# Up and gate products of four feed-forward layers in pairs by Strassen's scheme (Winograd's form)

## The chip, the cores and the metric

One core of one Trainium2 chip. The metric is the device time of one execution in microseconds, the median of the runs shown.

## The reference, cut to what matters

A float32 model on 512 tokens of width 1024: two hybrid layers (feed-forward, a mixer of delta rule, window attention and cross attention over 256 memory rows, feed-forward, each with a layer norm after it), then one block of another kind with four attentions and a convolutional feed-forward. The change touches the four feed-forward layers of the first part, in which `d_ff` is 2816:

```python
def swiglu(x, w_gu, w_down):
    gate, up = jnp.split(x @ w_gu, 2, axis=-1)
    return (jax.nn.silu(gate) * up) @ w_down
...
h = layer_norm(DEEPNORM_ALPHA * x + 0.5 * swiglu(x, ffn1_w_gu, ffn1_w_down), ln_g[0], ln_b[0])
...
return layer_norm(DEEPNORM_ALPHA * h + 0.5 * swiglu(h, ffn2_w_gu, ffn2_w_down), ln_g[2], ln_b[2])
```

## The kernel before, in words

Activations lie transposed, features on the partitions: an activation of width 1024 is 8 tiles ("pages", 128 partitions x 512 tokens), the hidden layer of a feed-forward 22. Weights come in blocks of 128 x 128. The precision of float32 is kept with rounded operands: each operand is split into a rounded part (`w_hi`, `X.hi`) and the rest (`w_lo`, `X.lo`), and a block is multiplied by three matmuls of 512 columns, hi x hi, hi x lo and lo x hi (`block_matmuls`, L2134, L2135, L2143). Eight PSUM banks hold the results.

The blocks of all layers form one stream, `weights`, in slabs of four blocks (`SLAB`, 256 KB). The program is made by a planner (`Order`) that runs once over the whole model and records every operation in the order in which each engine's queue then holds it. `place` (L478) hands out the next block and with it keeps the stream going: SP loads the slab 7 ahead (`load_slab`), ScalarE rounds the slab 4 ahead (`round_slab`, L2441), VectorE subtracts to get the rest, over the raw weights (`rest_slab`, L2822). The slab buffers are taken in turn: 7 raw ones and 5 rounded ones.

`ffn` (L771) goes over 22 pairs of output tiles, the gate tile j and the up tile 22 + j. Each is a `product` of 8 blocks into a bank. Two products later `ffn_act` turns the pair into one page of the hidden layer: ScalarE silu out of the gate's bank (L2512), VectorE times the up bank (L2969), ScalarE rounds (L2515), VectorE subtracts (L2972). `update` (L652) then multiplies by `down` (8 products of 22 blocks) and adds into the residual R (`add_up`, L2840). Norms and other side work are generators that step between the blocks (`Pace`); in the first feed-forward the norm of the memory rows and their key and value products (`prepare_memory`) run beside the up and gate products. `half_matmuls` (L2153 to L2155) is the last product of the program, in two halves of 256 columns.

```python
for m in range(len(open_pairs), FT):
    pair = []
    for n in (m, FT + m):
        if open_pairs:
            taken_in(j)
            j += 1
        pair.append(self.bg.straight(self.product(up, n, X), beside=True))
    open_pairs.append(pair)
```

Of the kernel before, what the change touches and what calls it, by code (L numbers as in the profile page):

```python
# [13 lines left out]
P = 128  # L14
# [19 lines left out]
NSLAB = 1120  # L34
NRAW = 7
NHI = 5
AHEAD = NHI - 1
# [3 lines left out]
PAGES = 82  # L41
CONST_PARTS = 4
NGAIN = 48

# [60 lines left out]
class Lane:  # L105
# [3 lines left out]
    def __init__(self, sems):  # L109
        self.tensor, self.scalar, self.vector = sems  # L110
        self.raised = [0, 0, 0]


class Marks(dict):
# [5 lines left out]
    def will(self, tensor="", scalar="", vector=""):  # L120
        lane = self.lane
        for k, (sem, names) in enumerate(((lane.tensor, tensor), (lane.scalar, scalar), (lane.vector, vector))):
            for name in names.split():
                lane.raised[k] += 1
                self[name] = (sem, lane.raised[k])
        return self


class Slot:
# [3 lines left out]
    def __init__(self, f, r=None):  # L133
        self.f, self.r, self.free, self.full = f, r, (), None

# [6 lines left out]

class Stock:


    def __init__(self, slots):
        self.slots = list(slots)

    def take(self):
        return self.slots.pop(0)  # L150

    def give(self, slot, *signals):
        slot.free = signals
        self.slots.append(slot)


class Operand:
# [3 lines left out]
    def __init__(self, tiles=None):  # L161
        self.tiles = tiles
        self.hi, self.lo, self.ready, self.pages = [], [], [], []

# [193 lines left out]
LANES = ("setup load norm ffn proj conv decay unit head0 head1 gate finish merge cross window soft0 soft1 "  # L358
# [3 lines left out]
class Memory:  # L362


    def __init__(self, nc, ctx, w, x_t, mem_t, consts, params, table, buckets, out):
# [5 lines left out]

        self.nc, self.w, self.x_t, self.mem_t, self.consts, self.params = nc, w, x_t, mem_t, consts, params
        self.table, self.buckets, self.out = table, buckets, out
        with nc.sbuf_tensor("w_lo", [P, NRAW, SLAB * P], F32R) as lo:
            self.w_lo = lo
        self.raw = sb("raw", [P, NRAW, SLAB * P])
        self.w_hi = sb("w_hi", [P, NHI, SLAB * P], F32R)
# [15 lines left out]
        self.lane_sems = {k: tuple(sem(f"{k}_{e}") for e in ("tensor", "scalar", "vector")) for k in LANES}  # L393
# [18 lines left out]
class Order:  # L412
# [5 lines left out]

    set_constants = load_constants = constants_ready = load_slab = round_slab = rest_slab = idle
# [19 lines left out]
    def __init__(self, memory):  # L439
# [3 lines left out]
        self.pages = Stock([Slot(f, r) for f, r in memory.page_aps])  # L443
        self.bg = Pace()
        self.order = []
        self.freed, self.multiplied = {}, 0
# [14 lines left out]

    def loaded(self, s):
        while self.next_raw <= min(s, NSLAB - 1):
            self.load_slab(self.next_raw)
            self.next_raw += 1

    def rounded(self, s):
        while self.next_round <= min(s, NSLAB - 1):
            self.round_slab(self.next_round)
# [3002 lines left out]
```

## Time and profile before

| what | value |
|---|---|
| time, median of 3 runs | 3622.58 us (3621.11 to 3623.22) |
| profiled execution: span | 3619.4 us |
| TensorE busy | 3578.4 us, 99% |
| weight loads busy | 2873.9 us, 79% |
| VectorE, ScalarE, GpSimd busy | 54%, 42%, 0% |
| DMA mean | 85 GB/s |

The times are of whole executions on the device. The profiled execution's own time is not listed beside them; what stands is its span, from its first to its last instruction, 3.2 us below the median. The page gives busy time by engine, a strip of 40 slices, the chain that ended last and the costliest groups of instructions; the trace can be asked for one line, one stretch or one engine in order of time. A matmul's end is modelled, and matmuls overlap, so the distance between two starts is what one costs.

### The profile page before, as it was taken

What the parts mean: (1) busy time and instruction counts of PE and PEld (TensorE: products, weight loads), DVE (VectorE), ACT (ScalarE), POOL (GpSimd) and SP (SyncE); (2) the same over time, 40 slices, a digit from 0 to 9 for tenths busy, and PEclk for the clock granted to TensorE, in tenths of its full rate; (3) what the DMA queues carried; (4) which work ended last, traced back from release to release, by engine and by line L of the source; (5) the groups of instructions that cost most, each with busy time, mean ns of one, the idle gap of its engine ahead of it and who ended that gap; (6) DMA issues with size and microseconds to landing.
All of it is one profiled execution on the core that took longest, in us unless ns stands there. A gap on an engine that the chain in (4) does not pass through costs nothing.

```text
span 3619.4 us, 44083 instructions
## 1 busy us (share of the span) xinstructions
PE 3578.4 (99%) x16952; PEld 2873.9 (79%) x16952; DVE 1945.8 (54%) x3781; ACT 1523.3 (42%) x2957; POOL 0.2 (0%) x4
## 2 busy tenths in 40 slices
PE   9999999999999999999999999999999999999999
PEld 7888878877888888888878877888886777788887
DVE  5333555556753345334655566733456787666643
ACT  4433354554443234333455543533335443444432
POOL 0000000000000000000000000000000000000000
PEclk9999999999999999999999999999999999999999
DMA  4443332112333333333321123333323222233333
GB/s 149 120 113 94 88 90 56 41 50 69 95 88 96 94 94 89 95 93 94 90 72 49 42 59 85 89 95 93 94 85 88 65 64 85 76 94 95 94 93 90
DMA packets 170600, 308.14 MB, mean 85 GB/s; under 512 B 19030, under 2 KB 23287, under 8 KB 170392
## 3 DMA queue, kind: packets, MB, share of 16 engines
q1 hardware_dynamic: 169624, 304.54, 29.8%
q8 instruction: 135, 2.21, 0.3%
q10 hardware_dynamic: 768, 0.79, 0.1%
q14 instruction: 73, 0.60, 0.1%
HBM read 300.27 MB, written 4.72 MB: 84 GB/s over the span
## 4 chain that ended last, share of the span: by engine, by line
PE 95%; DVE 2%; ACT 2%; issue 0%; DMA 0%; DVEq 0%; ACTq 0%
PE bank L2134 28%; PE bank L2143 28%; PE bank L2135 28%; PE bank L2122 2%; PE bank L2117 1%; PE bank L2195 1%; PE bank L2288 1%; PE bank L2298 1%; PE bank L2163 1%; PE bank L2215 0%; PE bank L2386 0%; PE bank L2208 0%; PE bank L2142 0%; PE bank L2236 0%; PE bank L2359 0%
## 5 line engine op out<-in xcount | busy, mean ns | idle before, releaser
L2134 PE MATMUL bank<-page_r,w_hi 128*128 128x512 f32 x4470 | 1788.1, 400 | 16.7 <-DVE w_lo L2822 9.6
L2143 PE MATMUL bank<-page_r,w_lo 128*128 128x512 f32 x4470 | 1765.9, 395 | 0.0
L2135 PE MATMUL bank<-page_r,w_hi 128*128 128x512 f32 x4470 | 1755.8, 393 | 0.0
L2441 ACT ACTIVATE w_hi<-raw 128x512 fp32r<-128x512 f32 x1120 | 697.2, 628 | 1022.0 <-PE bank L2143 1018.1
L2134 PEld LDWEIGHTS bank<-page_r,w_hi 128*128 128x128 f32 x4470 | 842.4, 188 | 220.6 <-issue 17.7
L2143 PEld LDWEIGHTS bank<-page_r,w_lo 128*128 128x128 f32 x4470 | 842.3, 188 | 191.9
L2135 PEld LDWEIGHTS bank<-page_r,w_hi 128*128 128x128 f32 x4470 | 842.2, 188 | 189.4 <-issue 3.6
L2822 DVE TENSOR_TENSOR w_lo<-raw,w_hi 128x512 fp32r<-128x512 f32 x1120 | 747.9, 687 | 417.8 <-ACT w_hi L2441 415.7
L2969 DVE TENSOR_TENSOR page_f<-page_f,bank 128x512 f32<-128x512 f32 x88 | 60.6, 688 | 322.6 <-PE bank L2143 276.1
L2840 DVE SCALAR_TENSOR_TENSOR page_f<-bank,page_f 128x512 f32<-128x512 f32 x64 | 44.2, 691 | 168.3 <-PE bank L2143 167.7
L2515 ACT ACTIVATE page_r<-page_f 128x512 fp32r<-128x512 f32 x88 | 55.7, 633 | 177.2 <-DVE page_f L2969 177.2
L2472 ACT ACTIVATE page_f<-page_f 128x512 f32<-128x512 f32 (+1 forms) x81 | 48.6, 604 | 126.9 <-DVE page_f L2840 113.4
L2569 ACT ACTIVATE page_f<-bank 128x256 f32<-128x256 f32 (+3 forms) x144 | 49.6, 388 | 123.8 <-PE bank L2122 123.4
L3291 DVE SCALAR_TENSOR_TENSOR page_f<-bank,par,page_f 128x511 f32<-128x511 f32 x88 | 65.4, 748 | 59.5 <-ACT page_f L2782 57.9
L2972 DVE TENSOR_TENSOR page_r<-page_f,page_r 128x512 fp32r<-128x512 f32 x88 | 60.9, 692 | 63.4 <-ACT page_r L2515 63.4
L2122 PE MATMUL bank<-cst,page_f 128*128 128x128 f32 x580 | 89.2, 275 | 5.7 <-DVE page_r L2828 4.7
L2122 PEld LDWEIGHTS bank<-cst,page_f 128*128 128x128 f32 x580 | 69.8, 143 | 23.7 <-DVE page_r L2828 5.5
L2977 DVE SCALAR_TENSOR_TENSOR page_f<-page_f,bank 128x512 f32<-128x512 f32 x80 | 54.8, 685 | 54.0 <-PE bank L2143 53.6
L2559 ACT ACTIVATE page_f<-bank 128x512 f32<-128x512 f32 x80 | 47.3, 592 | 54.0 <-PE bank L2143 53.8
L3045 DVE SCALAR_TENSOR_TENSOR page_f<-bank,par,page_f 128x511 f32<-128x511 f32 (+2 forms) x72 | 53.8, 748 | 23.7 <-ACT page_f L2611 22.0
L2195 PEld LDWEIGHTS bank<-page_f 128*64 128x64 f32 (+1 forms) x592 | 46.9, 148 | 23.1 <-issue 17.6
L2117 PE MATMUL bank<-page_f 128*128 128x128 f32 x512 | 65.2, 275 | 0.0
(251 smaller groups left out, 2507.4 us busy)
## 6 DMA issues: line engine op xcount, KB each, us to landing
raw<-weights SPq DMA_DIRECT2D x1120, 256.0 KB, 2.6
page_f<-x_t SPq DMA_DIRECT2D x8, 256.0 KB, 5.7
bias_rows<-page_f SPq DMA_DIRECT2D x8, 256.0 KB, 2.0
page_f<-bias_rows SPq DMA_DIRECT2D x8, 256.0 KB, 3.2
out_t<-page_f SPq DMA_DIRECT2D x12, 128.0 KB, 1.8
cst<-consts SPq DMA_DIRECT2D x4, 272.0 KB, 3.5
page_f<-mem_t SPq DMA_DIRECT2D x8, 128.0 KB, 3.3
bias_rows<-page_f SPq DMA_DIRECT2D x8, 64.0 KB, 1.9
```

What stands on the lines that cost most here:

```text
L2117: last = self.e.matmul(b.tile(i), x, y, start=True, stop=True)
L2122: last = self.e.transpose(b.tile(i), ap[:, i * P:(i + 1) * P], self.const("ident"))
L2134: self.e.matmul(o, hi, X.hi[kt], start=first, stop=False)
L2135: self.e.matmul(o, hi, X.lo[kt], start=False, stop=False)
L2143: last = self.e.matmul(o, lo, X.hi[kt], start=False, stop=final)
L2195: last = self.e.matmul(out.f[rows, i * P:(i + 1) * P], v, q.tile(kb), start=kb == 0, stop=kb == len(parts) - 1)
L2441: self.e.activation(self.m.w_hi[:, s % NHI, :], self.m.raw[:, s % NRAW, :], ACT.Copy) \
L2515: self.e.activation(h.r[:, :], s.f[:, :], ACT.Copy).then_inc(k.lane.scalar, 1)
L2822: self.e.tensor_tensor(self.m.w_lo[:, s % NRAW, :], self.m.raw[:, s % NRAW, :], self.m.w_hi[:, s % NHI, :].bitcast(F32), ALU.subtract).the ...
L2969: self.e.tensor_tensor(s.f[:, :], s.f[:, :], lift.f[:, :], ALU.mult).then_inc(k.lane.vector, 1)
L2972: self.e.tensor_tensor(l.r[:, :], s.f[:, :], h.r[:, :].bitcast(F32), ALU.subtract).then_inc(k.lane.vector, 1)
L3291: self.e.scalar_tensor_tensor(out=p.f[:, sh:], in0=b.f[:, 0:SEQ - sh], scalar=self.col("conv2", (2 - sh) * 2 * FT + m), in1=p.f[:, sh:], o ...
```

## The change

17 of the 22 pairs of each of the four layers (j = 5 to 21, 68 in all) are now made by Strassen's scheme in Winograd's form, in two stretches: 6 pairs, then the part of the `down` product that needs the hidden tiles 0 to 10, then 11 pairs, then the rest of `down`. The first 5 pairs stay as they were ("lone products").

For a pair the output is cut into 2 x 2: gate or up tile, tokens 0 to 255 or 256 to 511; the inner dimension is cut into k tiles 0 to 3 and 4 to 7. The weights are four quarters of 512 columns: a11 (gate, k 0 to 3), a21 (up, k 0 to 3), a22 (up, k 4 to 7), a12 (gate, k 4 to 7). There are 7 products of 4 blocks, each block 3 matmuls of 256 columns, where there were 16 blocks of 3 matmuls of 512:

- weights s1 = a21 + a22 and s3 = a21 + a11: one GpSimd instruction of 1024 columns, `sum_bottom`. s2 = s1 + a11 and s4 = s2 + a12: VectorE, 512 columns each (`sum_second`, `sum_fourth`). Signs lie in the sums of X.
- rounding on ScalarE: a11 (h11, 512 columns), s1 and s3 (h13), s2 and s4 (h24), a12 and a22 (h12), 1024 columns each. The rests on VectorE alike: l11, l13, l24, l12.
- sums of X, four per k tile, made once per layer (`sums_of`), in 16 pages.
- TensorE, in this order within a cycle: q1 (a11), q5 (s1), q4 of the pair before (a22), q6 (s2), q3 (s4), q2 (a12), q7 (s3). Products add up in PSUM: ScalarE copies q1 into q6's bank (`seed`), and keeps q5 (`p5`) and q6 (`u2`) in a page; VectorE adds `c12` (after q3) and `c22` (after q7, awaited by q4), multiplies with the two halves of silu (`h2`, `h1`), and ScalarE and VectorE round the page and take its rest.
- the preparation of a pair is cut into 9 steps (`prepare`), which stand between the products of the pair before and its own.

Raw buffers are 14 and rounded ones 9, of which 7 and 4 may be lent as pages; pages are 71 in place of 82. `prepare_memory` moves, with the loads of the constants and of the memory rows on SP, from the up and gate products of the first layer to the second part of its `down` product. The preparation of the first pair of a stretch (its "head") stands between the blocks of the last lone products, or of the first part of `down`.

```diff
-NSLAB = 1120
-NRAW = 7
-NHI = 5
+NSLAB = 1120 - 4 * 68
+NPAIR = 68
+NRAW = 14
+NHI = 9
+LOADED = 7
+LENT = {"raw": 7, "hi": 4}
-PAGES = 82
+PAGES = 71
...
+    def pair_product(self, p, name, bank, first, *after):
+        hi, lo, ready = p.units.pop(name)
+        p.k.will(tensor=name)
+        self.pair_matmuls(p.k, bank, first, hi, lo, ready, after, p.operands(name))
...
+            if cur:
+                k = cur.k
+                self.pair_product(cur, "q1", cur.a, True)
+            if prev:
+                self.pair_lift(prev.k, prev.b, prev.t)
+                self.pair_join(prev.k, prev.t, prev.s)
+            if cur:
+                step(cur)
+                self.pair_product(cur, "q5", cur.c, True)
+                self.pair_seed(k, cur.a, cur.b)
+                step(cur)
+            step(nxt)
+            if prev:
+                self.pair_product(prev, "q4", prev.b, False, prev.k["c22"])
+            if cur:
+                self.pair_keep(k, "p5", k["q5"], cur.c, cur.t, 0)
+                step(cur)
+                self.pair_product(cur, "q6", cur.b, False, k["seed"])
+            step(nxt)
+            if prev:
+                self.pair_last(prev.k, prev.b, prev.s)
+            if cur:
+                self.pair_product(cur, "q3", cur.c, False, k["p5"])
+                self.pair_keep(k, "u2", k["q6"], cur.b, cur.t, 1)
+            if prev:
+                self.pair_round(prev.k, prev.s, h)
+            step(nxt)
+            if cur:
+                self.pair_product(cur, "q2", cur.a, False, k["seed"])
+                self.pair_first(k, cur.c, cur.t, cur.s)
+            step(nxt)
+            if prev:
+                self.pair_rest(prev.k, prev.s, h, l)
+            if cur:
+                self.pair_product(cur, "q7", cur.b, False, k["u2"])
+                self.pair_gate(k, cur.a, cur.s)
+            step(nxt)
+            step(later)
...
+    def pair_matmuls(self, k, b, first, hi, lo, ready, after, xs):
+        for mark in after:
+            self.wait_ge(*mark)
+        self.wait_ge(*ready)
+        for kt, (x_hi, x_lo, x_ready) in enumerate(xs):
+            c = slice(kt * P, kt * P + P)
+            self.wait_ge(*x_ready)
+            self.e.matmul(b.cols(256), hi.r[:, c], x_hi, start=first and kt == 0, stop=False,
+                          skip_group_check=not first)
+            self.e.matmul(b.cols(256), hi.r[:, c], x_lo, start=False, stop=False, skip_group_check=not first)
+            last = self.e.matmul(b.cols(256), lo.r[:, c], x_hi, start=False, stop=kt == 3,
+                                 skip_group_check=not first)
...
+class Pool(Engine):
+    def sum_bottom(self, p, low, high, a21, out):
+        for unit in (low, high, a21):
+            self.wait_ge(*unit.full)
+        two = low.region.rearrange("p (u c) -> p u c", c=UNIT)[:, low.at:high.at + 1:step, :]
+        twice = a21.f.rearrange("p (o c) -> p o c", o=1).broadcast_to([P, 2, UNIT])
+        self.e.tensor_tensor(out[0].wide().rearrange("p (u c) -> p u c", c=UNIT), two, twice, ALU.add) \
```

VectorE's queue in the steady part of a layer's up and gate products, before (one pair; `page_f36` is the gate's page, `w_lo` a slab's rest, `blocks_multiplied` TensorE's count):

```order
L2822 TENSOR_TENSOR w_lo<-raw,w_hi 128x512 [waits slab_rounded] x7
L2969 TENSOR_TENSOR page_f36<-page_f36,bank4 128x512 [waits blocks_multiplied,ffn_scalar]
L2972 TENSOR_TENSOR page_r38<-page_f36,page_r37 128x512 [waits ffn_scalar,norm_vector]
L2822 TENSOR_TENSOR w_lo<-raw,w_hi 128x512 [waits slab_rounded] x8
L2969 TENSOR_TENSOR page_f76<-page_f76,bank1 128x512 [waits blocks_multiplied,ffn_scalar]
```

The same queue now, one cycle of the second stretch of the first layer (`prep_` and `pair_` are semaphores of the preparation and of the pairs; in order: second sum, l11, c12, fourth sum, rest of the page before, l13, c22, h2, l24 and l12, h1):

```order
L3215 TENSOR_TENSOR raw<-raw 128x512 [waits prep_pool]
L3230 TENSOR_TENSOR w_lo<-raw,w_hi 128x512 [waits prep_scalar]
L3259 TENSOR_TENSOR page_f36<-page_f26,bank7 128x256 [waits pair_scalar,pair_tensor]
L3221 TENSOR_TENSOR raw<-raw 128x512 [waits prep_vector,slab_landed6]
L3281 SCALAR_TENSOR_TENSOR page_r43<-page_f42,page_r37 128x512 [waits pair_scalar]
L3227 TENSOR_TENSOR w_lo<-raw,w_hi 128x1024 [waits prep_scalar]
L3264 TENSOR_TENSOR page_f26<-page_f26,bank1 128x256 [waits pair_tensor]
L3270 TENSOR_TENSOR page_f36<-page_f36,page_f26 128x256 [waits pair_vector,pair_scalar]
L3227 TENSOR_TENSOR w_lo<-raw,w_hi 128x1024 [waits prep_scalar] x2
L3276 TENSOR_TENSOR page_f36<-page_f36,bank1 128x256 [waits pair_tensor,pair_scalar]
```

Where a pair had four slab rests and two gate instructions of 512 columns, it now has eleven instructions, three of them of 1024 columns, and each waits for work of another engine or of its own in the same cycle.

ScalarE's queue in the same cycle (u2, round of the page before, h11, h13, silu of both halves, h24, h12, seed, p5):

```order
L2817 ACTIVATE page_f26<-bank1 128x256 [waits pair_tensor]
L2830 ACTIVATE page_r37<-page_f42 128x512 [waits pair_vector]
L2799 ACTIVATE w_hi<-raw 128x512 [waits slab_landed8]
L2797 ACTIVATE w_hi<-raw 128x1024 [waits prep_pool]
L2822 ACTIVATE page_f36<-page_f36 128x256 [waits pair_vector]
L2824 ACTIVATE page_f36<-bank2 128x256 [waits pair_tensor]
L2797 ACTIVATE w_hi<-raw 128x1024 [waits prep_vector]
L2797 ACTIVATE w_hi<-raw 128x1024 [waits slab_landed7,slab_landed6,pair_tensor]
L2812 ACTIVATE bank4<-bank5 128x256 [waits pair_tensor]
L2817 ACTIVATE page_f44<-bank3 128x256 [waits pair_tensor]
```

The round of the page and h11 now stand behind u2, and h13 ahead of the silu.

ScalarE's queue at the end of the first stretch (last p5 and u2, round of the page before, silu of both halves, round of the last page, then the slabs of the down product):

```order
L2817 ACTIVATE page_f42<-bank3 128x256 [waits pair_tensor]
L2817 ACTIVATE page_f42<-bank4 128x256 [waits pair_tensor]
L2830 ACTIVATE page_r52<-page_f70 128x512 [waits pair_vector,ffn_vector]
L2822 ACTIVATE page_f49<-page_f49 128x256 [waits pair_vector]
L2824 ACTIVATE page_f49<-bank0 128x256 [waits pair_tensor]
L2830 ACTIVATE page_r56<-page_f49 128x512 [waits pair_vector]
L2788 ACTIVATE w_hi<-raw 128x512 [waits slab_landed12]
L2788 ACTIVATE w_hi<-raw 128x512 [waits slab_landed10]
L2788 ACTIVATE w_hi<-raw 128x512 [waits slab_landed11]
```

The first slab of the down product is rounded only after the last pair's page. Before, slabs were rounded all the way from one product to the next.

## Rows read from the trace of the kernel before

**Rows 1.** The page, busy time by engine, and granted clock by slice

```profile
PE 3578.4 (99%) x16952; PEld 2873.9 (79%) x16952; DVE 1945.8 (54%) x3781; ACT 1523.3 (42%) x2957; POOL 0.2 (0%) x4
...
PEclk9999999999999999999999999999999999999999
```

**Rows 2.** The page, chain that ended last, by engine and by line

```profile
PE 95%; DVE 2%; ACT 2%; issue 0%; DMA 0%; DVEq 0%; ACTq 0%
PE bank L2134 28%; PE bank L2143 28%; PE bank L2135 28%; PE bank L2122 2%; PE bank L2117 1%; PE bank L2195 1%; PE bank L2288 1%; PE bank L2298 1%; PE bank L2163 1%; PE bank L2215 0%; PE bank L2386 0%; PE bank L2208 0%; PE bank L2142 0%; PE bank L2236 0%; PE bank L2359 0%
```

**Rows 3.** Groups by shape, TensorE: xcount | busy us, mean ns | idle before

```profile
L2134 PE MATMUL bank<-page_r,w_hi 128*128 128x512 f32 x4342 | 1752.1, 404 | 16.7 <-DVE w_lo L2822 9.6 <-DVE page_f L3026 3.2 <-DVE page_r L2964 2.5
```

**Rows 4.** Who waited for whom: us in total, times, longest us

```profile
ACT w_hi L2441 <- PE bank L2143: 1018.1, 607, 5.2
...
DVE page_f L2969 <- PE bank L2143: 276.1, 66, 6.1
```

**Rows 5.** Busy time of each engine, steady feed-forward stretch

```profile
core 0: us, PE busy (x) PEld busy (x) DVE busy (x) ACT busy (x) POOL busy (x), PEclk, DMA share, GB/s
1500.00:1600.00 100.00, 100.00 (x430) 80.53 (x429) 35.03 (x54) 31.21 (x53) 0.00 (x0) 1.00 0.34 95
```

**Rows 6.** Timeline, TensorE, last product: start us, us, line, form

```profile
3602.86 0.28 PE L2153 MATMUL bank<-page_r,w_hi 128*128 128x256 f32 x1
3602.97 0.28 PE L2154 MATMUL bank<-page_r,w_hi 128*128 128x256 f32 x1
...
3608.42 0.28 PE L2155 MATMUL bank<-page_r,w_lo 128*128 128x256 f32 x1
```

**Rows 7.** Timeline, weight loads, same product

```profile
3602.98 0.19 PEld L2155 LDWEIGHTS bank<-page_r,w_lo 128*128 128x128 f32 x1
3603.10 0.19 PEld L2153 LDWEIGHTS bank<-page_r,w_hi 128*128 128x128 f32 x1
```

**Rows 8.** Groups by shape, VectorE

```profile
L2822 DVE TENSOR_TENSOR w_lo<-raw,w_hi 128x512 fp32r<-128x512 f32 x1120 | 747.9, 687 | 417.8 <-ACT w_hi L2441 415.7
...
L2977 DVE SCALAR_TENSOR_TENSOR page_f<-page_f,bank 128x512 f32<-128x512 f32 x80 | 54.8, 685 | 54.0 <-PE bank L2143 53.6
...
L3026 DVE SCALAR_TENSOR_TENSOR page_f<-bank,cst 128x256 f32<-128x256 f32 x48 | 18.3, 420 | 66.0 <-PE bank L2215 66.0
```

**Rows 9.** Groups by shape, ScalarE

```profile
L2441 ACT ACTIVATE w_hi<-raw 128x512 fp32r<-128x512 f32 x1120 | 697.2, 628 | 1022.0 <-PE bank L2143 1018.1 <-DMA raw<-weights 3.2 <-issue 0.2
...
L2512 ACT ACTIVATE page_f<-bank 128x512 f32<-128x512 f32 x88 | 51.1, 581 | 0.1
...
L2569 ACT ACTIVATE page_f<-bank 128x256 f32<-128x256 f32 x92 | 31.6, 382 | 82.8 <-PE bank L2122 82.6
...
L2569 ACT ACTIVATE page_f<-bank 128x512 f32<-128x512 f32 x12 | 6.5, 596 | 8.6 <-PE bank L2122 8.6
```

**Rows 10.** Busy time of each engine, first stretch

```profile
0.00:53.00 53.00, 47.54 (x196) 38.27 (x197) 22.57 (x40) 26.19 (x44) 0.20 (x4) 1.00 0.59 184
```

**Rows 11.** Timeline, one steady gate, all engines

```profile
1199.52 0.40 PE L2134 MATMUL bank<-page_r,w_hi 128*128 128x512 f32 x1
...
1199.79 0.69 DVE L2969 TENSOR_TENSOR page_f<-page_f,bank 128x512 f32<-128x512 f32 x1 [4.25 <-PE bank L2143]
...
1200.51 0.63 ACT L2515 ACTIVATE page_r<-page_f 128x512 fp32r<-128x512 f32 x1 [2.42 <-DVE page_f L2969]
...
1201.05 0.61 ACT L2441 ACTIVATE w_hi<-raw 128x512 fp32r<-128x512 f32 x1
...
1201.24 0.69 DVE L2972 TENSOR_TENSOR page_r<-page_f,page_r 128x512 fp32r<-128x512 f32 x1 [0.77 <-ACT page_r L2515]
...
1201.85 1.29 DVE L2822 TENSOR_TENSOR w_lo<-raw,w_hi 128x512 fp32r<-128x512 f32 x2
```

**Rows 12.** DMA issues by line: KB each, median us to landing

```profile
raw<-weights SPq DMA_DIRECT2D x1120, 256.0 KB, 2.6
```

**Rows 13.** One line, L2155: durations, first and last start

```profile
L2155 PE MATMUL bank<-page_r,w_lo x20: 276/280/285, 3603.1 to 3610.3; 128*128 128x256 f32 x20
```

More of the change, by code:

```diff
@@ L40 @@
 HALF = (slice(0, 256), slice(256, 512))
-PAGES = 82
+PAGES = 71
 CONST_PARTS = 4
 NGAIN = 48
+UNIT = SLAB * P
+ALONE = 5
+FIRST = 11
+QUARTERS = ("a11", "a21", "a22", "a12")
 BLOCK_US = 0.7
@@ L772, in ffn @@
+    def ffn(self, source, X, up, down, scale, early, after, scaled=None, mem=None):
         H = Operand()
-        pairs = [m for j in range(3) for m in (j, FT + j)]
+        pairs = [m for j in range(ALONE) for m in (j, FT + j)]
+        self.until(len(pairs) * DT)
         if early:
             first = self.bg.got(self.bg.begin(source, X, [early.product(up, m) for m in pairs[:2]],
-                                              [self.product(up, m, X) for m in pairs[2:]], early.made))
+                                              [self.product(up, m, X) for m in pairs[2:6]], early.made))
@@ L793, in taken_in @@
             self.pages.give(s, k["rest"])
-        j = 0
-        for m in range(len(open_pairs), FT):
-            pair = []
+        if scaled:
+            self.bg.get(scaled)
+        sums = self.bg.add(self.sums_of(X, 1.0 / ALPHA))
+        head = self.pair(up, ALONE, FT + ALONE)
+        for m in range(len(open_pairs), ALONE):
+            made = []
             for n in (m, FT + m):
                 if open_pairs:
-                    taken_in(j)
-                    j += 1
-                pair.append(self.bg.straight(self.product(up, n, X), beside=True))
-            open_pairs.append(pair)
@@ L804, in ffn @@
-        while open_pairs:
-            taken_in(j)
-            j += 1
-        if scaled:
-            self.bg.get(scaled)
-        return self.update(down, H, scale, Spread(self, after, after.count == 2))
+                    taken_in()
+                w = Later(self.product(up, n, X))
+                while not w.done:
+                    self.bg.tell(w)
+                    self.bg.steps(1)
+                    if m == ALONE - 1 and not w.done and (n > FT or self.next_block % DT in (2, 5)):
+                        head.step(until=6)
@@ new lines, in ffn, with ahead @@
+                made.append(w.value)
+            open_pairs.append(made)
+        self.bg.get(sums)
+        while open_pairs:
+            taken_in()
+        def ahead(blocks):
+            self.until(blocks)
+            s = self.next_block // SLAB
+            for i in range(LOADED - 1):
+                self.loaded(s + i)
+            yield
+            self.rested(s + 2)
+        head.step(until=6)
+        self.paired(up, range(ALONE, FIRST), X, H, head, ahead(FIRST * DT))
+        part, H = H, Operand()
@@ new lines, in ffn @@
+        head = self.pair(up, FIRST, FT + FIRST)
+        left = FIRST * DT
+        for m in range(DT):
+            w = Later(self.product(down, m, part))
+            while not w.done:
+                self.bg.tell(w)
+                left -= 1
+                if left in (24, 20, 12, 9, 6, 3):
+                    head.step()
+            k = self.marks("norm").will(vector="sum")
+            self.add_up(k, w.value, m, scale)
+            self.Rt[m] = k["sum"]
+            self.banks.give(w.value, k["sum"])
@@ L811, in project @@
+        self.drop(part, w.value.full)
+        self.paired(up, range(FIRST, FT), X, H, head, ahead(NSLAB * SLAB))
+        self.drop(X, (self.lanes["pair"].tensor, self.lanes["pair"].raised[0]))
+        return self.update(down, H, scale, Spread(self, after, after.count == 2), k0=FIRST, beside=mem)
     def project(self, mat, mt, X, n=512, product=None):
@@ L3379, in _ @@
             Vector(e, memory).run()
-    return plan.order
+        @block.gpsimd
+        def _(e):
+            Pool(e, memory).run()
+    return plan.order, plan.pair_order
 def pad_cols(a, n):
```

433 lines of the change are left out of this document (371 added, 62 removed).

## The prediction

> **What bounds the kernel now.** I read the page's busy shares first: TensorE is busy for 3578.4 of 3619.4 us, VectorE for 54%, ScalarE for 42%, GpSimd not at all, and the granted clock is full in all 40 slices [rows 1]. The chain that ended last says the same: PE 95%, 28% on each of the three matmul lines [rows 2]. The groups by shape show that TensorE hardly waits: 16.7 us ahead of 4342 matmuls of the costliest form [rows 3]. So what counts is how many matmul columns are issued, and where TensorE is made to wait. The longest waits are ScalarE's and VectorE's for TensorE, 1018.1 us of one line [rows 4]: those engines have room, and idle time there is free.
>
> **The price of TensorE's work.** In steady feed-forward work 430 matmuls of 512 columns start in 100 us, 0.2326 us each, while VectorE is busy 35.03 us of the 100 [rows 5]. For 256 columns with a weight load before each, I take the last product: its first matmul starts at 3602.86 and the 48th at 3608.42, so 5.56/47 = 0.1183 us each [rows 6]. The loads there start 0.12 us apart and last 0.19, so they overlap one another [rows 7]; a load does not hold the short matmuls back.
> - Removed per pair: 16 blocks x 3 matmuls = 48 x 0.2326 = 11.16 us.
> - Added per pair: 7 products x 4 blocks x 3 = 84 x 0.1183 = 9.94 us, 1.42 per product.
> - 68 pairs x 1.225 = **-83.3 us** on the path. All other matmuls stay.
>
> **Does the rest keep up inside a stretch?** Prices [rows 8, 9]: VectorE 0.69 us for 512 columns, 0.42 for 256, so 1.04 ns a column and 1.22 for 1024 (an estimate from the two); ScalarE 0.63, 0.38 and, with 0.84 ns a column from its 596 and 382 ns, 1.06.
> - VectorE per pair: four of 512 (second sum, rest of a11, fourth sum, rest of the page) 2.76, three of 1024 (rests) 3.66, four of 256 (c12, c22, two multiplications) 1.68: 8.10 of 9.94 us, where before it had 35.03% of 11.16 = 3.9.
> - ScalarE: two of 512, three of 1024, five of 256: 6.34 us.
> - DMA: four quarters of 256 KB in 9.94 us, 105 GB/s; the start of the program ran at 184 [rows 10].
> - The sums of X, per layer: VectorE 4 x (4 x 0.42 + 2 x 0.69) = 12.2 us, under 10 lone products of 8 x 0.70 us. Cover 56 us, cost 0.
>
> Both fit in sum, but they are queues, so the tight loop has to be followed. Handovers come from one steady gate [rows 11]: TensorE to VectorE 0.27 us after the next product's first matmul (1199.52 to 1199.79), VectorE to ScalarE 0.03, ScalarE to VectorE 0.10; an instruction that is ready starts 0.08 (VectorE) or 0.09 (ScalarE) before the last one ends. From the end of q6: 0.27; u2 0.29; the previous pair's round 0.54; h11 of the next pair 0.63 + 0.10; on VectorE l11 0.61, c12 0.34, fourth sum 0.61, rest of the page 0.61, l13 1.22 + 0.03. That is 5.25 us, and only then may q5 of the next pair start. Between lie q3, q2, q7 and q1: 5.68 us. **Room 0.43 us**, cost 0; without any overlap it would be 5.75, 0.07 too long, over the 60 transitions (68 pairs less the first of each of 8 stretches) 4 us. The other handovers (seed, p5, c22, h1) have two products, 2.84 us, between writer and reader.
>
> **GpSimd's sum** has no row: the trace has only four memsets, 0.2 us together [rows 1]. Below it is bounded by VectorE's 1.22 us, above I allow four times that, 4.9; nearest is VectorE's row, and I take twice it, 2.4 us, for an engine that has only done memsets here. It waits for a22, whose transfer is issued when q7 of the pair before is done and takes 2.6 us [rows 12]: start at 2.8 us of the cycle, end 5.2, and the second sum has until 6.9. Cost 0. The Trainium skill (GPSIMD Engine Reference, Performance versus the Vector engine) has 4497 ns for an add of 2048 fp32 columns, thus an estimated 2.25 for this one; by it the sum is the same, and no run here shows it yet.
>
> **The ends of stretches** are where TensorE must wait; eight of them (6 and 11 pairs per layer, four layers). After the last q7, q4 waits for c22: 0.27 + 0.42 + 0.05 = 0.74. After q4 the down product waits for its first slab, whose rounding is queued behind the pair's own: 0.27, h1 0.42 + 0.03, round 0.54, slab round 0.63, then the slab's rest behind the page's rest on VectorE, which starts at 0.27 + 0.45 + 0.63 + 0.10 = 1.45 and lets the next one in 0.61 later: 2.06 + 0.69 + 0.05 = 2.8. Together 3.5 x 8 = **+28 us**; bounds 0 and 5 each. At the four entries after lone products the last gate (silu 0.58, times, round, rest) stands ahead of l24 and the seed: l24 ends 0.27 + 0.58 + 0.69 + 0.63 + 0.69 + 1.22 = 4.1 us after the last lone product, q6 could start at 2.84: 1.3 x 4 = **+5**. The entries from the middle of the down product have no gate: 0.
>
> **Once, in layer 1**: constants and memory (2.4 MB) are now queued on SP behind the last pair, and VectorE waits for them after five slab rests, 14 us of cover. At 184 GB/s [rows 10] they take 13 us, then the memory's norm starts, on whose mean TensorE waits: **+3**, bounds 0 and 8. Fewer pages (71, with 7 + 4 lent): 0, since the lenders are idle outside the stretches; if not, waits for pages would show in the mixers.
>
> **Sum**: 3619.4 - 83.3 + 28 + 5 + 3 = 3572.1 for the profiled execution; the median of the runs lies 3.2 above its span, thus **3575 us**.
>
> **The rivals.**
> 1. *VectorE and GpSimd hold each other up (slower).* If a GpSimd sum of length P starts at 2.8, just before l12, and VectorE must wait it out, then l12 (1.14), h1 (0.42 + 0.03) follow, and the round starts at P + 4.39 instead of 5.68 + 0.56 = 6.24. Less the room of 0.43 this costs P - 2.28 us per transition. At P = 2.4 that is 7 us in all; it decides from P = 3.06, where 60 x 0.78 eats the 47 won; at 3.5 it is 73 us, 3648. For it: VectorE would have 8.10 + P = more than 9.94 us. Against: l12 may get in first, then GpSimd waits instead and the room stays. It rests on the Trainium skill (SBUF — State Buffer, Who interferes with whom), which says that a VectorE instruction with two SBUF inputs and a GpSimd instruction reading SBUF block each other for the whole instruction; no row here can agree or not. Slower outright 12%; a milder form (P to 3, 3598 to 3618) 18%.
> 2. *The short matmuls do not reach 0.1183 us.* The stretch I took has no change of accumulator that waits. All sixty of that kind, from 3602.86 to 3610.3 [rows 6, 13], stand (3610.3 - 3602.86)/59 = 0.126 apart, with the norm's own matmuls and a wait among them. At that price: 68 x 84 x 0.0077 = 44 us more, 3619. Against it, the 47 intervals are even, and each block of four already changes its weights. 5%.
> 3. *The ends cost little*, if slabs were rounded earlier than the queues read: 3545. 6%.
> 4. *The products come, but the alone part stalls* for the sums or the heads, 5 us per layer: 3595. In the forecast's range.
>
> **How the numbers follow.** Forecast (TensorE the bound, 3552 to 3598) 59%, milder lock 18%, slower 12%, short matmuls 5%, cheap ends 6%. The range 3552 to 3616 leaves out the slower case and part of the cheap ends. A measurement of this kernel tells 0.2%, 7 us, from no change: faster by more (below 3615) 83%, within 5%, slower 12%.
>
> **What would show it.** 5712 matmuls of 256 columns on the pair line, 0.118 us apart; GpSimd with 68 instructions of some 2.4 us; VectorE busy about 80% in a stretch of pairs; TensorE's idle time, 41 us now, about 36 larger, at eight places of 3.5 us; a pair every 9.9 us. Wrong if the pair's period is 10.5 us or more, if VectorE's rests of 1024 last over 1.3 us while GpSimd is busy, or if TensorE idles before q5 or q7 in every pair.

## The result: the changed kernel is 0.17% slower, where 1.3% faster was predicted

| what | before | after |
|---|---|---|
| time, median of 20 runs each | 3622.07 us (3618.35 to 3623.91) | 3628.55 us (3624.96 to 3629.78) |
| ratio | | 1.0017, 95% interval 1.0011 to 1.0024 |
| profiled span | 3619.4 us | 3627.2 us |

The predicted time was 3575 us with a range of 3552 to 3616. The page of the changed kernel, busy time and clock, the chain that ended last, and the groups of TensorE's two first matmul lines (L2465 opens a block of 512 columns, L2500 one of 256 in a pair):

```profile
PE 3520.6 (97%) x19400; PEld 2952.2 (81%) x19400; DVE 2319.9 (64%) x4249; ACT 1691.5 (47%) x3259; POOL 200.9 (6%) x72
...
PEclk9999999999999999999999999999999999999999
...
PE 89%; DVE 7%; ACT 3%; issue 1%; DMA 0%; SPq 0%; DVEq 0%; ACTq 0%
...
L2465 PE MATMUL bank<-page_r,w_hi 128*128 128x512 f32 (+1 forms) x3382 | 1365.2, 404 | 45.1 <-DVE w_lo L3210 37.9
...
L2500 PE MATMUL bank<-page_r,w_hi 128*128 128x256 f32 x1904 | 539.7, 283 | 29.7 <-DVE w_lo L3230 15.1
```

Against [rows 1 to 3]: TensorE's share of the chain fell from 95% to 89%, VectorE's rose from 2% to 7%, and the idle time ahead of the two lines is 75 us where it was 17 ahead of one. In both cases what came last is a rest made by VectorE (`w_lo`). PE busy fell by 58 us, not by 83; part of the difference is slower work, below. Where does it wait? Windows of 100 us inside two stretches of pairs, with the columns of [rows 5]:

```profile
core 0: us, PE busy (x) PEld busy (x) DVE busy (x) ACT busy (x) POOL busy (x), PEclk, DMA share, GB/s
1200.00:1300.00 100.00, 100.00 (x847) 100.00 (x846) 85.10 (x110) 58.10 (x99) 28.71 (x9) 1.00 0.31 96
1020.00:1030.00 10.00, 10.00 (x44) 8.05 (x43) 9.85 (x15) 6.87 (x12) 0.00 (x0) 1.00 0.28 83
...
1060.00:1070.00 10.00, 4.95 (x23) 4.27 (x22) 8.55 (x10) 4.93 (x8) 2.41 (x1) 0.71 0.00 1
200.00:300.00 100.00, 99.01 (x837) 98.85 (x836) 84.05 (x109) 58.14 (x99) 27.57 (x9) 1.00 0.31 96
```

Inside a stretch it goes as foreseen: 847 matmuls start in 100 us, 0.118 us each, so a pair takes 84 x 0.118 = 9.9 us. The time is lost outside: from 1060 to 1070 us, where the second feed-forward layer goes from its lone products to its first pair, TensorE is busy for 4.95 us of 10, at a granted clock of 0.71. Forty microseconds earlier, where VectorE makes the norm beside the lone products, it is busy 9.85 us of 10 (6.45, 9.05, 9.85 and 4.96 in the four windows from 1000 to 1040 us). The timeline of TensorE at that entry (a number in brackets is idle time before, and what ended it):

```profile
1058.85 0.50 PE L2465 MATMUL bank<-page_r,w_hi 128*128 128x512 f32 x1 [1.19 <-DVE w_lo L3210]
...
1061.52 0.40 PE L2474 MATMUL bank<-page_r,w_lo 128*128 128x512 f32 x1
1066.96 0.55 PE L2500 MATMUL bank<-page_r,w_hi 128*128 128x256 f32 x1 [5.05 <-DVE w_lo L3230]
...
1067.75 0.41 PE L2500 MATMUL bank<-page_r,w_hi 128*128 128x256 f32 x1
1068.39 0.41 PE L2500 MATMUL bank<-page_r,w_hi 128*128 128x256 f32 x1
```

5.44 us lie between the last lone matmul and q1, and then one block of three takes 0.64 us instead of 0.355. With the wait at 1058.85 and a late q6 this entry costs 10.3 us, and the two in the other later layers 9.5 and 10.3. What VectorE and GpSimd do meanwhile (same timeline; L3238 to L3251 are the sums of X, L3428 and L3431 a lone gate, L3210 a slab's rest, L3215 the second sum, L3230 the rest of a11):

```profile
1047.60 0.41 DVE L3238 TENSOR_TENSOR page_f<-page_f 128x256 f32<-128x256 f32 x1
...
1051.64 1.29 DVE L3251 SCALAR_TENSOR_TENSOR page_r<-page_f,page_r 128x512 fp32r<-128x512 f32 x2
1052.85 0.69 DVE L3210 TENSOR_TENSOR w_lo<-raw,w_hi 128x512 fp32r<-128x512 f32 x1
...
1060.17 0.68 DVE L3428 TENSOR_TENSOR page_f<-page_f,bank 128x512 f32<-128x512 f32 x1
1061.55 0.69 DVE L3431 TENSOR_TENSOR page_r<-page_f,page_r 128x512 fp32r<-128x512 f32 x1 [0.70 <-ACT page_r L2903]
1062.05 2.41 POOL L3780 TENSOR_TENSOR raw<-raw 128x1024 f32<-128x1024 f32 x1 [15.53 <-PE bank L2474]
1062.16 3.45 DVE L3251 SCALAR_TENSOR_TENSOR page_r<-page_f,page_r 128x512 fp32r<-128x512 f32 x2
1065.54 0.68 DVE L3215 TENSOR_TENSOR raw<-raw 128x512 f32<-128x512 f32 x1
1066.14 0.68 DVE L3230 TENSOR_TENSOR w_lo<-raw,w_hi 128x512 fp32r<-128x512 f32 x1
```

VectorE is still making sums of X when the lone products are over. And one instruction pair, L3251 x2, takes 1.29 us at 1051.64 and 3.45 us at 1062.16, while GpSimd's sum runs. Groups by shape over the whole kernel:

```profile
L3227 DVE TENSOR_TENSOR w_lo<-raw,w_hi 128x1024 fp32r<-128x1024 f32 x204 | 309.0, 1542 | 0.0
L3780 POOL TENSOR_TENSOR raw<-raw 128x1024 f32<-128x1024 f32 x68 | 200.7, 2951 | 2404.6 <-PE bank L2474 1249.0 <-DMA raw<-pairs 866.2 <-PE bank L2503 289.4
...
L3251 DVE SCALAR_TENSOR_TENSOR page_r<-page_f,page_r 128x512 fp32r<-128x512 f32 x32 | 31.5, 1024 | 0.4 <-ACT page_r L2804 0.4
L3276 DVE TENSOR_TENSOR page_f<-page_f,bank 128x256 f32<-128x256 f32 x68 | 28.2, 415 | 28.8 <-PE bank L2503 28.8
```

Rests of 1024 columns (L3227) take 1.54 us on average where 1.22 was estimated. The last line is h1, which reads one operand from SBUF and one from a bank: 25 of its 68 executions lie wholly inside a GpSimd sum and take 420 to 422 ns, no more than others do. The end of a stretch (windows, then timeline; 1309.68 is the first block of the down product's second part in the second layer):

```profile
1306.90:1309.60 2.70, 0.21 (x2) 0.01 (x1) 1.69 (x4) 1.93 (x4) 0.00 (x0) 1.00 0.96 321
1310.00:1313.30 3.30, 3.30 (x9) 2.56 (x8) 2.04 (x4) 0.90 (x2) 0.00 (x0) 0.50 0.98 347
```

```profile
1309.68 0.61 PE L2465 MATMUL bank<-page_r,w_hi 128*128 128x512 f32 x1 [2.57 <-DVE w_lo L3210]
1310.94 0.63 PE L2465 MATMUL bank<-page_r,w_hi 128*128 128x512 f32 x1
1312.22 0.63 PE L2465 MATMUL bank<-page_r,w_hi 128*128 128x512 f32 x1
```

The wait is as forecast, eight times (L3210 makes the rest that ends it; L2788's rounding of the slab, at 1308.21 us, follows ScalarE's own last instruction without a wait for a transfer). But then the granted clock is 0.50, the lower of the two levels (1.2 in place of 2.4 GHz), and a block takes 1.27 us instead of 0.70. This follows six of the eight ends and costs some 1.5 us each.

### The profile page after: what moved, and what is told of

It is laid out like the page before. It is cut to its first block, busy times and chain, and to the rows that moved or that the text cites. A ratio compares the mean times of both kernels' runs of the same rounds, so it can differ in the third digit from the quotient of the medians.

```text
span 3627.2 us, 49995 instructions
## 1 busy us (share of the span) xinstructions
PE 3520.6 (97%) x19400; PEld 2952.2 (81%) x19400; DVE 2319.9 (64%) x4249; ACT 1691.5 (47%) x3259; POOL 200.9 (6%) x72
## 4 chain that ended last, share of the span: by engine, by line
PE 89%; DVE 7%; ACT 3%; issue 1%; DMA 0%; SPq 0%; DVEq 0%; ACTq 0%
PE bank L2465 21%; PE bank L2474 20%; PE bank L2466 20%; PE bank L2500 6%; PE bank L2503 5%; PE bank L2502 5%; PE bank L2453 2%; PE bank L2448 1%; PE bank L2543 1%; DVE w_lo L3227 1%; PE bank L2636 1%; DVE page_r L3251 1%; PE bank L2646 1%; DVE w_lo L3210 1%; PE bank L2511 1%
## 5 line engine op out<-in xcount | busy, mean ns | idle before, releaser
L2465 PE MATMUL bank<-page_r,w_hi 128*128 128x512 f32 (+1 forms) x3382 | 1365.2, 404 | 45.1 <-DVE w_lo L3210 37.9
L2474 PE MATMUL bank<-page_r,w_lo 128*128 128x512 f32 (+1 forms) x3382 | 1339.5, 396 | 0.0
L2466 PE MATMUL bank<-page_r,w_hi 128*128 128x512 f32 (+1 forms) x3382 | 1330.0, 393 | 0.0
L2465 PEld LDWEIGHTS bank<-page_r,w_hi 128*128 128x128 f32 x3382 | 641.5, 190 | 205.5 <-DVE w_lo L3210 44.0
L2788 ACT ACTIVATE w_hi<-raw 128x512 fp32r<-128x512 f32 x848 | 521.6, 626 | 598.3 <-PE bank L2474 593.9
L2466 PEld LDWEIGHTS bank<-page_r,w_hi 128*128 128x128 f32 x3382 | 641.5, 190 | 140.0 <-issue 3.6
L3210 DVE TENSOR_TENSOR w_lo<-raw,w_hi 128x512 fp32r<-128x512 f32 x848 | 563.0, 687 | 129.5 <-ACT w_hi L2788 129.1
L2500 PE MATMUL bank<-page_r,w_hi 128*128 128x256 f32 x1904 | 539.7, 283 | 29.7 <-DVE w_lo L3230 15.1
L2502 PE MATMUL bank<-page_r,w_hi 128*128 128x256 f32 x1904 | 537.5, 282 | 0.0
L2503 PE MATMUL bank<-page_r,w_lo 128*128 128x256 f32 x1904 | 537.3, 282 | 0.0
L2500 PEld LDWEIGHTS bank<-page_r,w_hi 128*128 128x128 f32 x1904 | 361.5, 190 | 34.8 <-issue 23.0
L2502 PEld LDWEIGHTS bank<-page_r,w_hi 128*128 128x128 f32 x1904 | 361.5, 190 | 0.2
L3780 POOL TENSOR_TENSOR raw<-raw 128x1024 f32<-128x1024 f32 x68 | 200.7, 2951 | 2404.6 <-PE bank L2474 1249.0
L3227 DVE TENSOR_TENSOR w_lo<-raw,w_hi 128x1024 fp32r<-128x1024 f32 x204 | 309.0, 1542 | 0.0
L2797 ACT ACTIVATE w_hi<-raw 128x1024 fp32r<-128x1024 f32 x204 | 213.2, 1054 | 27.4 <-DVE raw L3221 16.3
```

The costliest lines, as they stand in the source:

```text
L2465: self.e.matmul(o, hi, X.hi[kt], start=first, stop=False)
L2466: self.e.matmul(o, hi, X.lo[kt], start=False, stop=False)
L2474: last = self.e.matmul(o, lo, X.hi[kt], start=False, stop=final)
L2500: self.e.matmul(b.cols(256), hi.r[:, c], x_hi, start=first and kt == 0, stop=False, skip_group_check=not first)
L2502: self.e.matmul(b.cols(256), hi.r[:, c], x_lo, start=False, stop=False, skip_group_check=not first)
L2503: last = self.e.matmul(b.cols(256), lo.r[:, c], x_hi, start=False, stop=kt == 3, skip_group_check=not first)
```

## The experiments

Three causes stood out: the ends of stretches, the entries, and GpSimd's sum. Each was changed alone on the changed kernel (3628.55 us), then together. Times are medians; each ratio is to the kernel before, timed again with each group of runs (3622.55, 3623.25 and 3623.1 us), with its 95% interval.

**Ends: three slabs of the down product made earlier.** The generator `ahead` has two steps: it loads slabs, then it rounds three of them and takes their rests. They stood at the end of the last pair's cycle and at the end of the one behind it, which only finishes that pair. Now both stand inside the last pair's cycle, behind q4 of the pair before and ahead of q7:

```diff
+            if cur and not nxt:
+                next(ahead, None)
...
+            if cur and not nxt:
+                next(ahead, None)
             if cur:
                 self.pair_product(cur, "q7", cur.b, False, k["u2"])
...
-            if not nxt:
-                next(ahead, None)
```

> The first three slabs of the down product are loaded, rounded and rested inside the last pair's cycle, ahead of its q7, where they stood behind its page. Theory A (the stretches of pairs run as foreseen; what is lost stands at their ends and entries, each wait with a piece of half clock behind it): the 2.85 us between the last q4 and the first down block fall to under 0.5 at all eight ends, -20 to -22 us, and the pieces of half clock behind six of them go too, -1.5 us each, so some 3600 us. Theory B (VectorE is the bound and work that is put earlier comes back as another wait): under 5 us won, and q3, q7 or q4 of the last pairs start late instead.

Measured: 3597.41 us, ratio 0.9933 (0.992 to 0.9945), 31 less. TensorE at the first end (timeline): only the wait of q4 for c22 is left, and the down product (L2467) follows q4 (L2502 to L2505) at once.

```profile
127.22 0.42 DVE L3266 TENSOR_TENSOR page_f<-page_f,bank 128x256 f32<-128x256 f32 x1
...
127.70 0.39 PE L2502 MATMUL bank<-page_r,w_hi 128*128 128x256 f32 x1 [0.51 <-DVE page_f L3266]
...
129.10 0.28 PE L2505 MATMUL bank<-page_r,w_lo 128*128 128x256 f32 x1
129.22 0.40 PE L2467 MATMUL bank<-page_r,w_hi 128*128 128x512 f32 x1
```

So the 2.8 us behind each q4 come from where these steps stand in the queues, and the gap of 0.5 us that is left is followed by the full clock, eight times of eight. The entries stay at 10.6, 9.8 and 10.2 us.

**GpSimd's sum on VectorE.** `sum_bottom` as it stands, in VectorE's queue; GpSimd does nothing.

```diff
-        k.will(pool="bottom")
+        k.will(vector="bottom")
```

> The sum s1, s3 of each pair moves from GpSimd to VectorE; GpSimd does nothing. If GpSimd's reads stop VectorE's instructions with two SBUF inputs: the rests of 1024 columns fall from 1.54 us to 1.22, the five stalls of 1.2 us inside stretches go (6 us), and the three late entries lose 2 us each: -12 us, some 3616, although VectorE has 68 x 1.22 = 83 us more to do. If the long rests have another cause (ScalarE, DMA): they stay at 1.54, and VectorE's further 1.22 us per pair bring the pair's period over 9.94 us, 10 to 40 us slower.

Measured: 3602.86 us, ratio 0.995 (0.9938 to 0.9963), 26 less, though VectorE has 68 more instructions. By shape, the rests (first) and the sum (second):

```profile
L3238 DVE TENSOR_TENSOR w_lo<-raw,w_hi 128x1024 fp32r<-128x1024 f32 x204 | 242.8, 1218 | 0.0
L3220 DVE TENSOR_TENSOR raw<-raw 128x1024 f32<-128x1024 f32 x68 | 82.8, 1218 | 1.7 <-DMA raw<-pairs 1.5 <-issue 0.3
```

The rests fall from 1542 to 1218 ns: 204 x 0.324 = 66 us that VectorE had lost; the sum costs it 83. The direction was expected, the size was twice the expected one: the stalls in the middle of stretches (5 us) and the 1.1 us at the four entries from the down product went, the three late entries fell from 10 to 7 us, and the first layer's by 2. Another 4 us of the gain in the profiled execution is that three of the eight ends are followed by a piece of half clock, where six were; nothing in the edit explains that, so what the edit itself gives lies nearer 22 us than 26.

**Six lone pairs in place of five** (64 pairs by the scheme), on the changed kernel:

```diff
-ALONE = 5
+ALONE = 6
```

> Six lone pairs of output tiles per layer in place of five, 64 Strassen pairs in place of 68. It gives back 4 x 1.22 = 5 us of TensorE's gain and gives VectorE 7 us more per layer ahead of the first stretch. If the late entries (10 us each in three layers) come from VectorE's backlog of norm, sums of X and gates: q1 of the first stretch starts within 1 us of the last lone product, -7 to -9 us each, in sum 17 to 22 us faster than the change, some 3608. If they come from the loads of the head or from GpSimd alone: the entries stay near 10 us and it is 5 us slower, 3633.

Measured: 3618.02 us, ratio 0.9987 (0.9977 to 0.9996), 10.5 less, about half of what was expected. q1 now follows the last lone product without a gap, but the slabs' rests ahead of it come late (timeline):

```profile
1057.00 0.50 PE L2465 MATMUL bank<-page_r,w_hi 128*128 128x512 f32 x1 [2.10 <-DVE w_lo L3210]
...
1063.30 0.50 PE L2465 MATMUL bank<-page_r,w_hi 128*128 128x512 f32 x1 [0.43 <-DVE w_lo L3210]
```

VectorE's queue is full there, and one more lone pair moves part of the wait rather than removing it.

**TensorE kept busy behind q4.** 24 matmuls of 128 columns on a constant into a spare bank, behind the last q4, in all layers but the first; their results are used by nobody.

```diff
+            if prev and not cur and self.filling:
+                self.fill_matmuls(prev.k, spare, 24)
```

> 24 matmuls of 128 columns on a constant, into a spare bank, behind the last q4 of each stretch in all layers but the first (six ends); nothing else changes, and their results are used by nobody. They last 2.6 us at full clock, inside the wait of 2.85. If idleness lowers the clock: no piece of half clock behind those six ends (four have one now), -1.5 us each, some 6 us faster, 3622. If the clock falls for another reason: the same time, and the pieces stay.

Measured: 3620.54 us, ratio 0.9993 (0.9984 to 1.0002), 8 less. The slabs come no earlier, but after the fillers the clock stays up (window at the end that is shown above):

```profile
1309.00:1316.00 7.00, 7.00 (x32) 5.62 (x31) 2.41 (x5) 2.55 (x5) 0.00 (x0) 1.00 0.97 359
```

Two ends of the changed kernel, and both ends of the first layer in this run, which have no fillers, kept the full clock after the same idle time: it is not certain at each place, so one pair of traces proves little. All traces together say more. Of the 34 ends with 2.6 us of idle time in five traces (this one, the changed kernel, the sum on VectorE, six lone pairs, two steps), 19 are followed by a piece of half clock; of the six ends with fillers none; and none of the 56 in the seven traces whose slabs come earlier. So the half clock belongs to TensorE's idleness, and not to the transfers of some 350 GB/s that run with and without fillers. Of the 8 us, by the trace, some 6 are the four pieces that the fillers prevent, as expected; the two of the first layer are missing without them.

**Both edits together**, earlier slabs and the sum on VectorE:

> Both edits together: three down slabs prepared inside the last pair, and the bottom sum on VectorE (1218 ns) with GpSimd idle. If the losses are separate, the two gains add: 3628.5 - 31 - 26 = 3571 (3566 to 3578). If both edits mostly bought the same thing (the same VectorE backlog) or VectorE, now with 9.3 of 9.94 us per pair in a stretch, has no room for three more slab rests in the last pair: 3585 or more, with TensorE idle before q4 or in the middle of the last cycle.

Measured: 3572.1 us, ratio 0.9859 (0.9845 to 0.9872). The gains add up: -31.1 and -25.7 foretell 3571.7. The agreement is closer than the parts are known, since some 4 us of the second were the clock at ends that the first removes anyway; within that, the two causes are separate.

**Both edits and six lone pairs:**

> As the run with both edits, with 6 lone pairs and 16 made by the scheme in place of 5 and 17. Four pairs fewer cost 4 x 1.22 = +5 us. If the entries of the three later layers (7 us each there) are a backlog that two more lone products (11 us of cover) take away, -12 to -18: 5 to 12 us below the run with both edits. If the wait only moves to the slab rests ahead of the first pair, as in the run with 6 lone pairs alone, the two are within 3 us of each other.

Measured: 3563.21 us, ratio 0.9836 (0.9822 to 0.9849), 9 less again and 59 less than the kernel before. This is the best version found. TensorE's two lines on its page, against 45.1 and 29.7 us of idle time above:

```profile
L2467 PE MATMUL bank<-page_r,w_hi 128*128 128x512 f32 (+1 forms) x3446 | 1384.9, 402 | 20.3 <-DVE w_lo L3212 12.7
...
L2502 PE MATMUL bank<-page_r,w_hi 128*128 128x256 f32 x1792 | 504.6, 282 | 6.6 <-DVE page_f L3277 4.1
```

**Seven lone pairs, with both edits:**

> Both edits with 7 lone pairs and 15 by the scheme in each layer (60 in all). In the run with 6 lone pairs the entries of the later layers have 1.3 us of wait at slab rests and 0.86 at q6 left. If nothing more is to be gained there, this one shows the price of a pair alone: 4 x 1.22 = 4.9 us more, 3568; if the 1.3 us go as well, 3564. A price of a pair under 1 us would give 3563 to 3567 and speak against the first term of the prediction.

Measured: 3569.27 us, ratio 0.9852 (0.9836 to 0.9867), 6.1 more for four pairs fewer. That is 1.5 us for each pair where the prediction had 1.22, and above both expected values. The trace has the same waits ahead of and at the entries as the one with six lone pairs, so nothing more was gained there, and 1.9 of its 6.1 us are one more piece of half clock (at 1831.5 us, between the third and the fourth feed-forward layer). What is left, some 4 us, is near the price of four pairs, 4.9.

**The side work two steps at a block**, on the changed kernel and on the version with both edits:

```diff
                     self.bg.tell(w)
-                    self.bg.steps(1)
+                    self.bg.steps(2)
```

> The changed kernel with the side work two steps at a block, alone, GpSimd and ends untouched. With the order theory 5 to 15 us less than 3628.5, the entries of the three later layers shorter by 2 to 5 us each; with the amount theory no change within 3 us, the wait at slab rests around 1058 us growing by what the entry loses.

> As the run with both edits, but the side work beside the lone products is let forward two steps at a block in place of one, so that the sums of X stand nearer the norm and leave the queue ahead of the first pair's preparation earlier. If what delays the entries is that the sums come late: 5 to 12 us less. If it is VectorE's whole amount of work between norm and first pair, order does not help: the same within 3 us, or more, where slab rests now stand behind the sums.

Measured: 3629.7 us alone, ratio 1.002 (1.0011 to 1.0029), so no gain; with both edits 3588.09, ratio 0.9901 (0.9888 to 0.9915), 16 us worse than 3572.1. Against the run with both edits the wait at q1 shrinks from 4.0 to 0.46 us, but rests come late ahead of it and q6 behind it (timeline, the second of these versions):

```profile
1042.82 0.50 PE L2467 MATMUL bank<-page_r,w_hi 128*128 128x512 f32 x1 [2.58 <-DVE w_lo L3212]
...
1053.48 0.36 PE L2502 MATMUL bank<-page_r,w_hi 128*128 128x256 f32 x1 [0.46 <-DVE w_lo L3243]
...
1058.90 0.36 PE L2502 MATMUL bank<-page_r,w_hi 128*128 128x256 f32 x1 [2.06 <-DVE w_lo L3240]
```

My theory of order fell here: with this order the waits only change places. That does not make order unimportant, for this one costs 16 us, and on the changed kernel VectorE is busy only 4.96 us of 10 from 1030 to 1040 us, just ahead of the sums. The two runs with a sixth lone pair show that more lone products ahead of the first pair help. No other order was tried.

**GpSimd beside VectorE, with nobody waiting for it.** The sum on VectorE left open whether GpSimd had hurt by holding VectorE up or as a slow link that others wait for. On the best version, GpSimd now adds an area of its own to itself beside each bottom sum. Nothing reads it. A control does the same with 16 columns.

```diff
-PAGES = 71
+PAGES = 69
...
+    def beside(self, p, low, high, a21, last):
+        for unit in (low, high, a21):
+            self.wait_ge(*unit.full)
+        s = self.m.spare[:, :].rearrange("p (u c) -> p u c", c=UNIT)
+            self.e.tensor_tensor(s, s, s, ALU.add).then_inc(p.prep.lane.pool, 1)
```

> The version with both edits and 6 lone pairs (3563.2), all sums on VectorE, and beside each bottom sum one GpSimd add of 1024 columns on an area of its own, which nobody reads and nobody waits for (67 of them; pages 69 in place of 71). If a GpSimd instruction and VectorE's hold each other up by themselves, VectorE's rests of 1024 columns go from 1.22 us back to 1.4 or more on average, GpSimd's add takes over 2.4 us, TensorE waits in the middle of stretches again, and the time is 15 us or more over 3563. If GpSimd only hurt as a slow link in the chain of the preparation, nothing changes: 3563 within 3 us.

> The control to the run with the unused GpSimd adds: the same program with the same 69 pages and waits, but each GpSimd add has 16 columns. Both theories: 3563 within 3 us, VectorE's rests at 1.22 us. If this one is slower too, the pages or GpSimd's waits were the cause and not its reading and writing.

Measured: 3609.42 us, ratio 0.9963 (0.9951 to 0.9976), with 1024 columns, and 3565.07, ratio 0.9841 (0.9827 to 0.9854), with 16. By shape, with 1024 columns: rests, GpSimd's add, VectorE's sum, then two instructions of 256 columns, h2 with both operands from SBUF and c22 with one from a bank:

```profile
L3246 DVE TENSOR_TENSOR w_lo<-raw,w_hi 128x1024 fp32r<-128x1024 f32 x192 | 277.7, 1473 | 0.0
...
L3796 POOL TENSOR_TENSOR spare<-spare 128x1024 f32<-128x1024 f32 x63 | 142.5, 2262 | 2397.7 <-DMA raw<-pairs 2397.7
L3228 DVE TENSOR_TENSOR raw<-raw 128x1024 f32<-128x1024 f32 x64 | 89.6, 1400 | 1.1 <-PE bank L2511 1.1
L3289 DVE TENSOR_TENSOR page_f<-page_f 128x256 f32<-128x256 f32 x64 | 46.6, 728 | 7.0 <-ACT bank L2820 0.5
L3283 DVE TENSOR_TENSOR page_f<-page_f,bank 128x256 f32<-128x256 f32 x64 | 26.6, 416 | 3.0 <-PE bank L2511 2.9
```

and with 16:

```profile
L3246 DVE TENSOR_TENSOR w_lo<-raw,w_hi 128x1024 fp32r<-128x1024 f32 x192 | 228.9, 1220 | 0.0
...
L3228 DVE TENSOR_TENSOR raw<-raw 128x1024 f32<-128x1024 f32 x64 | 78.3, 1223 | 0.7 <-DMA raw<-pairs 0.7
L3796 POOL TENSOR_TENSOR spare<-spare 128x16 f32<-128x16 f32 x63 | 30.8, 489 | 2460.3 <-DMA raw<-pairs 2460.3
L3289 DVE TENSOR_TENSOR page_f<-page_f 128x256 f32<-128x256 f32 x64 | 27.3, 426 | 7.0 <-DVE page_f L3283 0.5
L3283 DVE TENSOR_TENSOR page_f<-page_f,bank 128x256 f32<-128x256 f32 x64 | 26.7, 418 | 3.7 <-PE bank L2511 3.7
```

A result that nobody wants costs 46 us (44 against the control): GpSimd holds VectorE up by its long reading and writing beside it. It is a matter of the operands: of two instructions of the same shape and stage, h2 goes from 426 to 728 ns, while c22 takes 418 and 416. VectorE's rests and sums are 192 x 0.253 + 64 x 0.177 = 60 us longer, and h2 64 x 0.302 = 19. Most of it reaches TensorE; the windows of the best version and of the one with GpSimd's adds, over the same stretch, show why:

```profile
200.00:300.00 100.00, 99.49 (x838) 99.15 (x837) 81.75 (x118) 56.29 (x99) 0.00 (x0) 1.00 0.38 118
```

```profile
200.00:300.00 100.00, 95.33 (x781) 94.17 (x781) 91.74 (x111) 53.58 (x93) 21.08 (x9) 0.98 0.30 90
```

VectorE goes from 82% to 92% busy with fewer instructions, and TensorE starts 57 matmuls fewer, about a quarter of them by a piece of half clock (0.98 in this window). GpSimd's add was expected at over 2.4 us; it is 2.26 on average.

## Why the prediction was wrong, step by step

Excesses are worked out from the distances of TensorE's starts against its steady ones.

| term | predicted | measured |
|---|---|---|
| pairs in place of products | -83.3 | -83, from a period of 9.9 us |
| ends of stretches | +28 | +38 |
| entries | +5 | +39 |
| stalls in the middle of stretches | 0 | +5 |
| first layer's constants and memory | +3 | +8 |
| the mixers and the last block | 0 | +5 |

The measured terms sum to +12 against a span that grew by 7.8; the 4 us between are not placed. Of the 55 us between the predicted span (3572.1) and the measured one, the entries are 34.

- **The pairs' price was right.** 0.118 us per short matmul and 9.94 us per pair hold. Rival 2 is out.
- **The room in the loop was right, by luck in part.** Its 8.10 us of VectorE work came out as 85.10% of 9.94 = 8.5, with held-up rests in it. (The order shown for VectorE before the change is from the first layer, where the memory's products stand between the gates; in the other layers four rests lie between two gates, as the text beside it says.) The luck: in most cycles a rest had begun before GpSimd's sum, in many by 0.13 us only, so that the sum waited first. The prediction named this as possible and could not know it. Four times GpSimd got ahead of l24 and l12, and q6 came 1.2 us late; in one of them (235.77 us) the sum took 2.51 us beside two rests of 4.55 together, where two take 2.35.
- **Rival 1, the lock, was real, but at other places than where I priced it.** It was to decide from a sum of 3.06 us per transition; the sum took 2.95 on average and the period did not move. The rival's test, rests over 1.3 us, came out at 1.54. By the run without it the lock cost 22 to 26 us, mostly at entries and heads, where VectorE's queue was full already. The Trainium skill (SBUF — State Buffer, Who interferes with whom) calls the ports that VectorE shares with GpSimd an exclusive lock, and says that a VectorE instruction with two SBUF inputs contends with a GpSimd instruction that reads SBUF, while one with at most one SBUF input, outside the 2-port modes, does not. The trace agrees on both: L3251 x2 is held from 1.29 to 3.45 us, while h1 (L3276, one input from a bank) takes 415 ns on average, and 416 without GpSimd's sum. The 4497 ns for 2048 columns of the Trainium skill (GPSIMD Engine Reference, Performance versus the Vector engine) gave an estimate of 2.25 us; the shortest sum of the changed kernel took 2.39.
- **The ends' wait was right and incomplete.** 0.7 before q4 and 2.85 behind it are the 3.5 of the sum, 28 us in all. What was left out is the half clock that follows: 10 us more. No term was set for what a wait does to the clock. The prediction took the clock of the kernel before for full in all 40 slices, but a 9 there stands for 90% or more: the mean is 0.996, and its trace has five stretches of half clock.
- **The step that failed is the entries: "12.2 us, under 10 lone products of 8 x 0.70 us. Cover 56 us, cost 0", and 1.3 us per entry.** The price of the sums was right, the cover was not. Six of the ten lone products run while VectorE makes the norm (up to 9.85 us busy of 10), and norm, slab rests, gates, sums and head share one queue. In the later layers the sums have 22 us at most, with lone gates and eight slab rests in them. I had summed VectorE's work for the pair's cycle and for no other window. The first layer, whose input needs no norm, lost 4.8 us; the later ones 10 each. Rival 4 named this mechanism, "the alone part stalls for the sums or the heads", at 5 us per layer, and left it inside the forecast's range without a chance of its own; its place was right, its size half of what the three later layers show. The entries from the down product were put at 0 and cost 1.1 each, by the lock, since they vanish with the sum on VectorE.
- **First layer's memory:** inside its bounds of 0 to 8. TensorE waits 3.3 us for the memory path's ScalarE copy at 358 us, with a half clock behind it. Moving that work was not tried.
- The version with both edits lands at 3572.1 us, near the predicted 3575. That is chance, for its terms are others: ends at 6 in place of 28, entries at some 23 in place of 5.

## What to carry to other kernels

When one engine is made cheaper, add up the work of the next engine window by window, with what the neighbouring stage already puts into its queue; a cover counts only for the stretch in which that engine is free. Prepare the operands of the next stage inside the last cycle of this one: it was a move of a few lines, worth 31 of 3628 us. Don't put work on GpSimd to relieve a busy VectorE whose instructions read two operands from SBUF: of 83 us of sums taken off it, 66 came back as held-up time in the rests alone, and the version with the sums on VectorE was 26 us faster.

## What the runs showed of the hardware

- A GpSimd add of 1024 columns that nobody reads costs this kernel 44 us over its 16-column control; VectorE's rests of 1024 columns, with two inputs from SBUF, go from 1.22 to 1.47 us on average over all of them, and h2 (256 columns, two from SBUF) from 426 to 728 ns; c22 (256 columns, one from SBUF and one from a bank) takes 418 and 416.
- Behind 2.6 us of idle time TensorE's granted clock fell to 0.50 in six of eight cases in the changed kernel, and in 19 of 34 over five traces; there a block of three matmuls of 512 columns takes 1.27 us and not 0.70. With 24 matmuls of 128 columns in that idle time it stayed at 1.00, six times of six, and behind gaps of 0.5 us 56 times of 56.
- Two causes of waiting, 31 and 26 us when removed one at a time, gave 56 us when both were removed.
